# Neighbourhood attention in pairs of heads: two heads' scores on two row tiles, values stationary in two column tiles, probabilities normalised before they are turned

## The chip, the core and the metric

The program runs on one core of a Trainium2 chip. The metric is the device time of one launch in microseconds. Shares, waits and rows come from one profiled execution of the kernel before.

## What is computed

A trunk of four layers over 256 tokens of width 1024, all in float32: state-space mixer, short convolution, neighbourhood attention, state-space mixer, each followed by a squared-ReLU MLP of width 4096 and each sub-layer by a layer norm. The change lies in the attention of the third layer. There the tokens form a grid of 4 rows by 64 columns, there are 16 heads of 64 features, and a query attends to 16 columns of all four rows:

```python
def na_mixer(x, w_qkv, rpb, w_out):
    qkv = (x @ w_qkv).reshape(bsz, rows, GRID_W, 3, NA_HEADS, NA_HEAD_DIM)
    q = qkv[:, :, :, 0] * (NA_HEAD_DIM ** -0.5)
    k = qkv[:, :, :, 1]
    v = qkv[:, :, :, 2]
    ...
    bias = rpb[:, dr_idx[:, None, None, :, None], dc_idx[None, :, :, None, :]]
    bias = jnp.where(in_win[None, None, :, :, None, :], bias.astype(jnp.float32), -jnp.inf)
    def one(t):
        ...
        s = jnp.einsum('rcqhd,rcikhd->hrcqik', qb, kg).astype(jnp.float32) + bias
        p = jax.nn.softmax(s.reshape(shp[:4] + (shp[4] * shp[5],)), axis=-1).reshape(shp)
        o = jnp.einsum('hrcqik,rcikhd->rcqhd', p.astype(vs.dtype), vg)
        return o.reshape(rows * GRID_W, NA_HEADS * NA_HEAD_DIM)
    return lax.map(one, (q, k, v)) @ w_out
```

## The kernel before

Weights stream through in units of 128x2048 numbers. SyncE loads a unit into one of 3 raw buffers, ScalarE copies it to w_high in a rounded float32 form (fp32r), VectorE subtracts to get w_low (the rest), and TensorE multiplies with high and low parts (three matmuls for one product). There are 4 split buffers: the split of unit u waits until unit u-4 has been used, and `result(u)` on ScalarE and VectorE first does the splits up to unit u+3 and then waits for unit u's product. Each engine has its own instruction queue, executed in order and written out by hand; semaphores tie them together.

The attention stage takes the 1024 columns of q, k and v in four blocks of four heads (units q, k, v for each block; v first in block 0), and then four units "no" of the output projection, which accumulate in the four y banks of PSUM. Besides those there are two acc banks, used in turn by the projections of q, k and v, and two inner banks.

For a head, TensorE runs `scores` (q of 128 positions stationary, 64 features contracted, moving 160 keys; twice, for the two halves z of the grid's columns), VectorE adds the bias, takes the maximum and negates it (`biased`, up to L1937), ScalarE writes exp and its sum (`exponents`, L1438) into prob_b (in the tensor xsT, two buffers, a head's number mod 2), TensorE turns the probabilities (`turn_probs`, L1022), ScalarE copies them to SBUF (`keep_probs`, L1449, probT_b in the tensor conv, two buffers), and TensorE mixes the values (`mix_values`, L1033: turned probabilities stationary, 64 features of v moving). ScalarE scales the result by the inverse sum (`scale_out`, L1459) into o_b. After four heads TensorE turns the outputs (`turn_out`, L1047) and ScalarE and VectorE write the high and low part of the operand of the output projection (`out_high` L1468, `out_low` L1950).

TensorE's order for head h is scores(h), dense(h), turn_probs(h-1), mix_values(h-2), and turn_out after heads 7, 11 and 15. dense(h) is a share of the projections: 2, 2, 1, 1 halves of a unit for the heads of a block, for blocks 1 to 3 while heads 0 to 11 run; then half units of "no" 0 and 1 for heads 12 to 15. ScalarE's order is exponents(h), then `keep_qkv` for each unit that dense(h) completed (splits up to u+3, then a copy to ring_a, ring_b or ring_c), from head 14 the split of a further unit, then keep_probs(h-1), scale_out(h-2), out_high. VectorE's is biased(h), the splits, sum_inverse(h-1) (L1942), out_low.

The banks for scores, turned probabilities, mixed values and turned outputs are taken in turn from a ring: inner 0 and 1 and y 0 to 3 up to head 11, inner 0 and 1 and acc 0 and 1 from head 12. Each taking waits until the bank's last content has been read (`take`, called at L551). At head 12 the acc banks are marked as free once qkv_done has reached 12, that is after the copy of the last v. The wait for the probability buffer stands in `exponents`:

```python
                        act.wait_ge(s_max, h + 1)
                        if h >= 2:

                            act.wait_ge(pt_ready, h - 1)
```

## Time and profile before

| | us |
|---|---|
| median of 3 runs | 1497.29 |
| the runs | 1497.29, 1500.34, 1493.65 |
| span of the profiled execution, first to last instruction | 1494.3 |
| TensorE busy in it | 1431.1 (96%) |
| VectorE busy | 999.5 (67%) |
| ScalarE busy | 770.8 (52%) |
| GpSimd busy | 197.1 (13%) |

No other time of the profiled execution is recorded than its span; the runs were timed apart from it.

PE in the profile is TensorE's matmuls, PEld its weight loads, DVE VectorE, ACT ScalarE, POOL GpSimd. Matmuls are pipelined: the duration shown of one reaches past the start of the next, so what a stream costs is read from the distance of its starts. A float32 product is carried out as two instructions each with a weight load, a float32 turning and an fp32r product as one.

### The profile page before, as it was taken

What the parts mean: (1) busy time and instruction counts of PE and PEld (TensorE: products, weight loads), DVE (VectorE), ACT (ScalarE), POOL (GpSimd) and SP (SyncE); (2) the same over time, 40 slices, a digit from 0 to 9 for tenths busy, and PEclk for the clock granted to TensorE, in tenths of its full rate; (3) what the DMA queues carried; (4) which work ended last, traced back from release to release, by engine and by line L of the source; (5) the groups of instructions that cost most, each with busy time, mean ns of one, the idle gap of its engine ahead of it and who ended that gap; (6) DMA issues with size and microseconds to landing.
All of it is one profiled execution on the core that took longest, in us unless ns stands there. A gap on an engine that the chain in (4) does not pass through costs nothing. (4 is left out here: it accounts for less than half of the span.)

```text
span 1494.3 us, 24586 instructions
## 1 busy us (share of the span) xinstructions
PE 1431.1 (96%) x9723; PEld 1325.6 (89%) x9723; DVE 999.5 (67%) x1229; ACT 770.8 (52%) x1105; POOL 197.1 (13%) x245
## 2 busy tenths in 40 slices
PE   7899998999999999999999999999998999999996
PEld 7889997989989989998899889998988999899995
DVE  5899899555487575555744465456789898955554
ACT  4786775344434334444455535443577777454441
POOL 2223222622320000000000000000033121200000
PEclk9999999999999999999999999999999999999998
DMA  8666554666666454556553245645657564555550
GB/s 242 201 197 225 168 172 141 177 191 211 209 199 222 155 192 168 198 176 208 184 166 113 86 141 179 215 170 178 197 170 227 173 191 144 169 179 188 198 197 28
DMA packets 198192, 266.96 MB, mean 179 GB/s; under 512 B 11768, under 2 KB 167824, under 8 KB 198080
## 3 DMA queue, kind: packets, MB, share of 16 engines
q1 hardware_dynamic: 188720, 237.72, 48.0%
q0 software_dynamic: 9200, 27.55, 6.1%
q8 instruction: 78, 1.28, 0.4%
q14 instruction: 34, 0.28, 0.1%
q10 hardware_dynamic: 160, 0.13, 0.0%
HBM read 264.19 MB, written 1.18 MB: 178 GB/s over the span
## 5 line engine op out<-in xcount | busy, mean ns | idle before, releaser
L587 PE MATMUL acc<-xT,w_high 128*128 128x256 f32 x3264 | 599.9, 286 | 3.4 <-DVE w_low L1527 3.4
L1527 DVE TENSOR_TENSOR w_low<-raw,w_high 128x2048 fp32r<-128x2048 f32 (+1 forms) x226 | 512.1, 2275 | 89.4 <-ACT w_high L1119 55.0
L1119 ACT ACTIVATE w_high<-raw 128x2048 fp32r<-128x2048 f32 (+1 forms) x226 | 427.1, 1896 | 208.4 <-DMA raw<-in_ffn_w_in 82.4
L587 PEld LDWEIGHTS acc<-xT,w_high 128*128 128x128 f32 x3264 | 515.7, 193 | 8.7 <-issue 4.9
L587 PE MATMUL acc<-xT,w_low 128*128 128x256 f32 x1632 | 464.0, 284 | 0.0
L739 PE MATMUL y<-w_high,opT 128*128 128x512 f32 x1408 | 398.1, 392 | 1.1 <-ACT w_high L1119 1.0
L587 PEld LDWEIGHTS acc<-xT,w_low 128*128 128x128 f32 x1632 | 315.4, 193 | 0.0
L739 PEld LDWEIGHTS y<-w_high,opT 128*128 128x128 f32 x1408 | 260.0, 189 | 52.4 <-ACT w_high L1119 1.1
L739 PE MATMUL y<-w_low,opT 128*128 128x512 f32 x704 | 223.4, 391 | 0.0
L1546 DVE TENSOR_TENSOR opT<-conv,opT 128x512 fp32r<-128x512 f32 x56 | 39.2, 701 | 264.9 <-issue 238.0
L608 PE MATMUL acc<-w_high,xT 128*128 128x256 f32 (+1 forms) x928 | 177.4, 293 | 9.5 <-DVE xT L1591 9.5
L608 PEld LDWEIGHTS acc<-w_high,xT 128*128 128x128 f32 x928 | 150.4, 199 | 13.0 <-issue 12.7
L739 PEld LDWEIGHTS y<-w_low,opT 128*128 128x128 f32 x704 | 132.6, 188 | 28.4
L608 PE MATMUL acc<-w_low,xT 128*128 128x256 f32 (+1 forms) x464 | 134.2, 289 | 0.0
L430 POOL TENSOR_TENSOR small<-small,minus_half 128x1 f32<-128x1 f32 x16 | 15.9, 993 | 827.0 <-DVE small L1567 827.0
L1162 ACT ACTIVATE conv<-acc 128x512 f32<-128x512 f32 x60 | 35.9, 598 | 147.2 <-PE acc L587 133.0
L1663 DVE SCALAR_TENSOR_TENSOR conv<-conv_pad,ssd_par,conv 128x256 f32<-128x256 f32 x256 | 107.1, 489 | 4.4 <-ACT conv L1193 4.4
L608 PEld LDWEIGHTS acc<-w_low,xT 128*128 128x128 f32 x464 | 92.2, 199 | 0.0
L1149 ACT ACTIVATE xT<-inner 128x512 fp32r<-128x512 f32 x32 | 18.1, 596 | 98.9 <-PE inner L709 98.6
L453 POOL TENSOR_TENSOR ring_a<-ring_b,decay_to_end 128x512 f32<-128x512 f32 x16 | 27.6, 1727 | 161.0 <-ACT ring_b L1249 156.8
L453 POOL TENSOR_TENSOR ring_b<-ring_b,own_token 128x512 f32<-128x512 f32 x16 | 44.3, 2771 | 32.2 <-DVE own_token L1714 32.2
L526 POOL DMA_DIRECT2D E<-in_na_rpb x64 | 34.1, 539 | 95.6 <-ACT conv L1162 94.5
(221 smaller groups left out, 1196.6 us busy)
## 6 DMA issues: line engine op xcount, KB each, us to landing
raw<-in_ffn_w_in SPq DMA_DIRECT2D x128, 512.0 KB, 4.7
raw<-in_ffn_w_out SPq DMA_DIRECT2D x128, 512.0 KB, 4.4
raw<-in_ssd_w_in SPq DMA_DIRECT2D x96, 512.0 KB, 5.3
E<-cumsum_dram POOLq DMA_DIRECT2D x32, 512.0 KB, 6.1
raw<-in_ssd_w_out SPq DMA_DIRECT2D x32, 512.0 KB, 4.4
raw<-in_sc_w_in SPq DMA_DIRECT2D x24, 512.0 KB, 4.8
raw<-in_na_w_qkv SPq DMA_DIRECT2D x24, 512.0 KB, 4.7
raw<-in_sc_w_out SPq DMA_DIRECT2D x8, 512.0 KB, 4.5
```

What stands on the lines that cost most here:

```text
L430: nc.gpsimd.tensor_tensor(small[:, 2 + t:3 + t], small[:, t:t + 1], half_neg[:, 0:1], ALU.pow).then_inc(rstd_done, 1)
L453: return nc.gpsimd.tensor_tensor(spread(dst, shape), spread(tri_b[:, n % 2, :], shape), factors, ALU.mult)
L526: pool.dma_start(dst, src).then_inc(window_landed[h % WINDOW_BUFS], 16)
L587: mm = nc.tensor.matmul(bank[:, c * SEQ:(c + 1) * SEQ][:, span], w[:, col:col + P], xT[:, k, low, span], start=(k == 0 and part == 0), sto ...
L608: mm = nc.tensor.matmul(bank[:, t * width:(t + 1) * width], xT[:, k, low, t * P:(t + 1) * P], w[:, k * width:(k + 1) * width], start=(k == ...
L739: mm = nc.tensor.matmul(Y[t][c][:, :], opT[:, o % ACTS, low, k, t * P:(t + 1) * P], w[:, k * D + c * 512:k * D + (c + 1) * 512], start=(fi ...
L1119: nc.scalar.activation(w_high[:, u % SPLIT, c0:k * c], raw[:, u % RAW, c0:k * c], ACT.Copy).then_inc(w_high_done, 1)
L1149: nc.scalar.activation(xT[:, 4 * half:4 * half + 4, 0, t * P:(t + 1) * P], bank[:, :].rearrange("p (k c) -> p k c", k=4), ACT.Copy).then_i ...
L1162: nc.scalar.activation(conv[:, o % 2, :, :], views(bank[:, :]), ACT.Relu).then_inc(relu_done, 1)
L1527: V.tensor_tensor(w_low[:, u % SPLIT, c0:k * c], raw[:, u % RAW, c0:k * c], f(w_high[:, u % SPLIT, c0:k * c]), ALU.subtract).then_inc(w_lo ...
L1546: V.tensor_tensor(low, src, high, ALU.subtract).then_inc(op_low, 1)
L1663: ins = V.scalar_tensor_tensor(out=y, in0=pad[:, c % 2, i, q:q + SEQ], scalar=tap(j, q, ct), in1=y, op0=ALU.mult, op1=ALU.add)
```

## The change

Heads go in pairs p = 0 to 7. `scores(p)` takes two banks and issues for each z head 2p (rows 0 to 63 of the array) and head 2p+1 (rows 64 to 127). `mix_values(p)` now holds v (64 columns) stationary and moves 256 positions of the turned probabilities, head 2p into output partitions 0 to 63 and head 2p+1 into 64 to 127 of one bank. `turn_out`, `scale_out` and o_b go. The inverse sum is multiplied into the probabilities on VectorE before they are turned (`normalised`), and turn_probs waits for that instead of for the exponents. `out_high` and `out_low` run once for a pair on half an operand. dense(p) has 4, 2, 4, 2, 4, 2 half units and then twice the two halves of "no" 0 and 1. The order of the three queues is written anew by pairs; `exponents` and `biased` keep their waits except that `biased` no longer waits for o_done.

```diff
--- before.py
+++ after.py
@@ -120,16 +120,17 @@
     return units, subs
+PAIRS = NAH // 2
 def attention_order():
     halves = [(what, b, part) for b in range(1, 4) for what in QKV_ORDER[1] for part in range(2)]
-    share = (2, 2, 1, 1) * 3
...
+    plan = [[halves.pop(0) for _ in range(n)] for n in (4, 2) * 3]
+    return plan + [[("no", b, part) for part in range(2)] for b in range(2)]
+ATT_DENSE = attention_order()
 def silu_count(kind, m):
@@ -274,7 +275,8 @@
         qkv_done = sem("qkv_done")
         s_ready, s_biased, s_max, p_done = sem("s_ready"), sem("s_biased"), sem("s_max"), sem("p_done")
-        pt_ready, pt_done, o_ready, o_done = sem("pt_ready"), sem("pt_done"), sem("o_ready"), sem("o_done")
+        pt_ready, pt_done, o_ready = sem("pt_ready"), sem("pt_done"), sem("o_ready")
+        o_half_high, o_half_low = sem("o_half_high"), sem("o_half_low")
         bias_done, prob_zeroed, p_scale = sem("bias_done"), sem("prob_zeroed"), sem("p_scale")
         act_step, dve_step, pool_step = sem("act_step"), sem("dve_step"), sem("pool_step")
...
@@ -1003,54 +1004,48 @@
                     late_ring = [("i", 0), ("i", 1), ("a", 0), ("a", 1)]
                     pe.wait_ge(y_free, 2 * s)
-                    def scores(h):
-                        blk, hh = h // BLOCK_HEADS, h % BLOCK_HEADS
+                    def scores(p):
+                        blk, c = p // 2, (p % 2) * SEQ
                         pe.wait_ge(qkv_done, 3 * blk + (2 if blk else 3))
-                        bank = inner_bank(("s", h), (s_biased, h + 1), ring)
-                        rows, c = slice(64 * (hh % 2), 64 * (hh % 2) + 64), (hh // 2) * SEQ
-                        k = tri_b[rows, blk % 3, c:c + SEQ].rearrange("p (r c) -> p r c", c=GRID_W)
+                        banks = [inner_bank(("s", h), (s_biased, h + 1), ring) for h in (2 * p, 2 * p + 1)]
                         for z in range(2):
-                            mm = nc.tensor.matmul(bank[:, z * KEYS:(z + 1) * KEYS], tri_a[rows, blk % 3, c + z * P:c + (z + 1) * P],
...
+                            for i in range(2):
+                                rows = slice(NAD * i, NAD * (i + 1))
+                                k = tri_b[rows, blk % 3, c:c + SEQ].rearrange("p (r c) -> p r c", c=GRID_W)
+                                mm = nc.tensor.matmul(banks[i][:, z * KEYS:(z + 1) * KEYS], tri_a[rows, blk % 3, c + z * P:c + (z + 1) * P],
+                                                      k[:, :, col0[z]:col0[z] + KCOLS], start=True, stop=True)
+                                if z:
+                                    mm.then_inc(s_ready, 1)
+                    def turn_probs(p):
+                        for h in (2 * p, 2 * p + 1):
+                            pe.wait_ge(p_scale, h + 1)
+                            bank = inner_bank(("pt", h), (pt_done, h + 1), ring)
+                            for t in range(NT):
+                                for z in range(2):
+                                    mm = nc.tensor.transpose(bank[:, t * SEQ + z * P:t * SEQ + (z + 1) * P],
+                                                             prob_b[h % 2][:, z * SEQ + t * P:z * SEQ + (t + 1) * P], ident[:, :])
+                            mm.then_inc(pt_ready, 1)
+                    def mix_values(p):
+                        blk, c = p // 2, p % 2
+                        o = n["op"] + blk
+                        pe.wait_ge(qkv_done, 3 * blk + 3)
+                        pe.wait_ge(pt_done, 2 * p + 2)
+                        bank = inner_bank(("o", p), (op_low, o + 1) if c else (o_half_low, blk + 1), ring)
                         for t in range(NT):
-                            for z in range(2):
...
+                            for i in range(2):
+                                v0 = t * COLS + (2 * c + i) * NAD
+                                mm = nc.tensor.matmul(bank[NAD * i:NAD * (i + 1), 0:SEQ], tri_c[:, blk % 3, v0:v0 + NAD],
+                                                      probT_b[i][:, t * SEQ:(t + 1) * SEQ], start=(t == 0), stop=(t == NT - 1))
                         mm.then_inc(o_ready, 1)
...
-                    def dense(h):
-
-                        for what, blk, part in ATT_DENSE[h]:
+                    def dense(plan):
+                        for what, blk, part in plan:
                             if what == "no":
                                 out_half(s, names[(what, blk)], part, blk == 0)
                             else:
@@ -1059,35 +1054,40 @@
                     banks = {}
                     for what in "qk":
                         project(names[(what, 0)], range(NT))
-                    for h in range(NAH):
-                        if h == 12:
+                    for p in range(PAIRS - 1):
+                        if p == 6:
                             ring = late_ring
                             for b in range(2):
                                 freed[("a", b)] = (qkv_done, 12)
-                        scores(h)
...
+                        scores(p)
+                        dense(ATT_DENSE[p])
+                        if p >= 1:
+                            turn_probs(p - 1)
+                        if p >= 2:
+                            mix_values(p - 2)
+                    scores(PAIRS - 1)
+                    dense(ATT_DENSE[PAIRS - 1][:1])
+                    turn_probs(PAIRS - 2)
+                    mix_values(PAIRS - 3)
+                    dense(ATT_DENSE[PAIRS - 1][1:])
+                    turn_probs(PAIRS - 1)
+                    mix_values(PAIRS - 2)
                     out_half(s, names[("no", 2)], 0, False)
-                    turn_out(3)
+                    mix_values(PAIRS - 1)
                     out_half(s, names[("no", 2)], 1, False)
                     tail(s, [names[("no", 3)]])
-                if kind in ("ffn", "conv"):
+                if kind != "ssd":
                     n["op"] += FFN // COLS if kind == "ffn" else 4
-        def reversed_tokens(bank):
+        def in_token_order(bank):
             ap = bank[:, :]
-            return bass.AP(ap.tensor, ap.offset + SEQ - 1, [list(ap.ap[0]), [SEQ, 2], [-1, SEQ]])
+            return bass.AP(ap.tensor, ap.offset + SEQ - 1, [list(ap.ap[0]), [-QCOLS, ROWS], [-P, 2], [-1, QCOLS]])
+        def by_grid(operand):
+            return operand.rearrange("p (r z c) -> p r z c", r=ROWS, z=2)
         def tap(j, q, ct):
@@ -1413,7 +1413,7 @@
                         bank = result(names[(what, b)])
                         if b == 3:
-                            act.wait_ge(o_ready, BLOCK_HEADS)
+                            act.wait_ge(o_ready, 2)
                         dst = {"q": tri_a, "k": tri_b, "v": tri_c}[what][:, b % 3, :]
                         if what == "q":
                             for c in range(2):
@@ -1441,52 +1441,40 @@
                                                        accum_out=att[:, h % 4, 4 + z:5 + z])
                         ins.then_inc(p_done, 1)
-                    def keep_probs(h):
...
-                    base = n["turned"]
+                    def keep_probs(p):
+                        for h in (2 * p, 2 * p + 1):
+                            act.wait_ge(pt_ready, h + 1)
+                            if p:
+                                act.wait_ge(o_ready, p)
+                            nc.scalar.activation(probT_b[h % 2], inner_of[("pt", h)][:, :], ACT.Copy).then_inc(pt_done, 1)
+                    def out_high(p):
+                        c = p % 2
+                        act.wait_ge(o_ready, p + 1)
+                        nc.scalar.activation(by_grid(operand(n["op"])[:, c, :]), in_token_order(inner_of[("o", p)]),
+                                             ACT.Copy).then_inc(op_high if c else o_half_high, 1)
+                        n["op"] += c
                     for what in QKV_ORDER[0]:
                         keep_qkv(what, 0)
-                    for h in range(NAH):
-                        exponents(h)
-                        for what, b, part in ATT_DENSE[h]:
+                    for p in range(PAIRS):
+                        for h in (2 * p, 2 * p + 1):
+                            exponents(h)
+                        for what, b, part in ATT_DENSE[p]:
                             if part and what != "no":
                                 keep_qkv(what, b)
-                        if h >= 14:
...
+                        if p >= 6:
+                            split_to(names[("no", 3)] + p - 6)
+                        if p >= 1:
+                            keep_probs(p - 1)
+                        if p >= 2:
+                            out_high(p - 2)
+                    keep_probs(PAIRS - 1)
+                    out_high(PAIRS - 2)
+                    out_high(PAIRS - 1)
             split_to(len(units) - 1)
@@ -1927,43 +1915,46 @@
                         if h >= 2:
                             dve.wait_ge(p_done, h - 1)
-                        if h >= 4:
-
-                            dve.wait_ge(o_done, h - 3)
                         V.scalar_tensor_tensor(out=sc, in0=inner_of[("s", h)][:, 0:2 * KEYS], scalar=float(NAD) ** -0.5,
                                                in1=bias_all[:, h, :], op0=ALU.mult, op1=ALU.add).then_inc(s_biased, 1)
                         dve.wait_ge(s_biased, h + 1)
                         chain(V.tensor_reduce(st[:, 0:2], views(sc), AX.X, ALU.max))
                         V.tensor_scalar(st[:, 2:4], st[:, 0:2], -1.0, None, ALU.mult).then_inc(s_max, 1)
-                    def sum_inverse(h):
+                    def normalised(h):
                         st = att[:, h % 4, :]
                         dve.wait_ge(p_done, h + 1)
-                        V.reciprocal(st[:, 6:8], st[:, 4:6]).then_inc(p_scale, 1)
-
...
+                        chain(V.reciprocal(st[:, 6:8], st[:, 4:6]))
+                        shape = [[SEQ + col0[1] - col0[0], 2], [GRID_W, ROWS], [1, KCOLS]]
+                        probs = spread(prob_b[h % 2][:, col0[0]:col0[0] + 1], shape)
+                        V.tensor_tensor(probs, probs, spread(st[:, 6:7], [[1, 2], [0, ROWS], [0, KCOLS]]), ALU.mult).then_inc(p_scale, 1)
+                    def out_low(p):
+                        c, o = p % 2, n["op"]
+                        dve.wait_ge(*((op_high, o + 1) if c else (o_half_high, p // 2 + 1)))
                         low, high = operand(o)
-                        V.tensor_tensor(low, reversed_tokens(inner_of[("op", o)]), high, ALU.subtract).then_inc(op_low, 1)
+                        V.tensor_tensor(by_grid(low[:, c, :]), in_token_order(inner_of[("o", p)]), by_grid(high[:, c, :]),
+                                        ALU.subtract).then_inc(op_low if c else o_half_low, 1)
+                        n["op"] += c
                     for what in QKV_ORDER[0]:
                         split_to(names[(what, 0)] + 3)
-                    for h in range(NAH):
-                        biased(h)
-                        for what, b, part in ATT_DENSE[h]:
+                    for p in range(PAIRS):
+                        for h in (2 * p, 2 * p + 1):
+                            biased(h)
+                        for what, b, part in ATT_DENSE[p]:
                             if part and what != "no":
                                 split_to(names[(what, b)] + 3)
-                        if h >= 14:
...
+                        if p >= 6:
+                            split_to(names[("no", 3)] + p - 6)
+                        for h in (2 * p, 2 * p + 1):
+                            normalised(h)
+                        if p >= 2:
+                            out_low(p - 2)
+                    out_low(PAIRS - 2)
+                    out_low(PAIRS - 1)
             for t in range(NT):
                 norm(len(subs) - 1, t)
```

## Rows read from the trace of the kernel before

**Rows 1.** The page: busy time and share of TensorE's matmuls.

```profile
PE 1431.1 (96%) x9723; PEld 1325.6 (89%) x9723; DVE 999.5 (67%) x1229; ACT 770.8 (52%) x1105; POOL 197.1 (13%) x245
```

**Rows 2.** Busy us by engine over the stage, instructions, granted clock, DMA share, GB/s.

```profile
746.70:855.70 109.00, 107.61 (x776) 99.35 (x777) 47.98 (x81) 59.85 (x141) 0.00 (x0) 0.98 0.38 126
```

**Rows 3.** Timeline of TensorE, a head's step: start, length, line, output and inputs, count.

```profile
803.63 0.28 PE L587 MATMUL acc<-xT,w_high 128*128 128x256 f32 x1
803.75 0.28 PE L587 MATMUL acc<-xT,w_low 128*128 128x256 f32 x1
803.87 0.60 PE L1022 MATMUL inner<-ident,xsT 128*128 128x128 f32 x4
804.30 1.00 PE L1033 MATMUL inner<-ring_c,conv 128*128 128x64 f32 x8
805.24 0.81 PE L1013 MATMUL y<-ring_b,ring_a 64*128 64x160 f32 x4
```

**Rows 4.** Timeline of TensorE, turned outputs, scores, a half unit of output projection.

```profile
796.74 0.61 PE L1047 MATMUL y<-ident,gate 128*128 128x128 f32 x4
...
823.26 0.61 PE L1047 MATMUL y<-ident,square 128*128 128x128 f32 x4
823.80 0.81 PE L1013 MATMUL inner<-ring_b,ring_a 64*128 64x160 f32 x4
824.54 0.73 PE L739 MATMUL y<-w_high,opT 128*128 128x512 f32 x2
...
827.39 0.60 PE L1022 MATMUL inner<-ident,xsT 128*128 128x128 f32 x4
```

**Rows 5.** The scores' line: length in ns of one (least, median, most).

```profile
L1013 PE MATMUL y<-ring_b,ring_a x32: 296/296/400, 753.5 to 818.8; 64*128 64x160 f32 x32
```

**Rows 6.** Timeline of TensorE in the last layer: float32 products of 256 moving columns.

```profile
1262.17 1.03 PE L884 MATMUL inner<-ring_a,E 128*128 128x256 f32 x4
1263.04 1.89 PE L897 MATMUL inner<-ring_b,E 128*128 128x64 f32 x16
```

**Rows 7.** Timeline of ScalarE over a head's exponents, a split, copies.

```profile
800.78 0.43 ACT L1438 ACTIVATE xsT<-tanh,softmax_stats 128x160 f32<-128x160 f32 x1 [2.33 <-DVE softmax_stats L1937]
...
801.62 1.90 ACT L1119 ACTIVATE w_high<-raw 128x2048 fp32r<-128x2048 f32 x1
804.07 0.66 ACT L1423 ACTIVATE ring_a<-acc 128x256 f32<-128x256 f32 x2 [0.55 <-PE acc L587]
804.61 0.60 ACT L1449 ACTIVATE conv<-inner 128x512 f32<-128x512 f32 x1
```

**Rows 8.** Timeline of VectorE over a split, an inverse and a head's bias and maximum.

```profile
803.60 2.29 DVE L1527 TENSOR_TENSOR w_low<-raw,w_high 128x2048 fp32r<-128x2048 f32 x1 [2.86 <-ACT w_high L1119]
805.81 0.15 DVE L1942 RECIPROCAL softmax_stats<-softmax_stats 128x2 f32<-128x2 f32 x1
806.08 0.49 DVE L1933 SCALAR_TENSOR_TENSOR tanh<-y,E 128x320 f32<-128x320 f32 x1
...
807.13 0.17 DVE L1937 TENSOR_SCALAR softmax_stats<-softmax_stats 128x2 f32<-128x2 f32 x1
```

**Rows 9.** Timeline of TensorE at the stage's end; in brackets idle time and its releaser.

```profile
845.51 1.08 PE L1033 MATMUL acc<-ring_c,conv 128*128 128x64 f32 x8 [0.90 <-ACT conv L1449]
846.85 1.08 PE L1033 MATMUL acc<-ring_c,conv 128*128 128x64 f32 x8 [0.26 <-issue]
848.08 0.81 PE L739 MATMUL y<-w_high,opT 128*128 128x512 f32 x2
...
852.50 0.60 PE L1047 MATMUL inner<-ident,square 128*128 128x128 f32 x4
852.85 0.71 PE L739 MATMUL y<-w_high,opT 128*128 128x512 f32 x2
```

**Rows 10.** Timeline of TensorE in the last layer, behind its longest idle stretch.

```profile
1151.43 0.41 PE L897 MATMUL inner<-ring_b,E 128*128 128x64 f32 x2 [3.04 <-DVE E L1708]
```

**Rows 11.** By stretch as in rows 2: the clock behind those two idle stretches.

```profile
849.00:852.00 3.00, 3.00 (x8) 2.31 (x8) 0.00 (x0) 0.00 (x0) 0.00 (x0) 0.51 0.91 316
1152.00:1159.00 7.00, 7.00 (x36) 7.00 (x36) 6.97 (x9) 2.17 (x2) 3.75 (x3) 0.52 0.82 295
```

More of the change, by code:

```diff
@@ L120, in plan_units @@
     return units, subs
+PAIRS = NAH // 2
 def attention_order():
     halves = [(what, b, part) for b in range(1, 4) for what in QKV_ORDER[1] for part in range(2)]
-    share = (2, 2, 1, 1) * 3
-    plan = [[halves.pop(0) for _ in range(n)] for n in share]
-    plan += [[("no", b, part)] for b in range(2) for part in range(2)] + [[]]
-    return plan, {7: 0, 11: 1, 15: 2}
-ATT_DENSE, ATT_TURN = attention_order()
+    plan = [[halves.pop(0) for _ in range(n)] for n in (4, 2) * 3]
+    return plan + [[("no", b, part) for part in range(2)] for b in range(2)]
+ATT_DENSE = attention_order()
 def silu_count(kind, m):
@@ L1965, in _ @@
-                    sum_inverse(NAH - 1)
-                    out_low()
+                        if p >= 6:
[6 more added lines that the diff above has]
+                    out_low(PAIRS - 1)
             for t in range(NT):
```

84 lines of the change are left out of this document (removed).

## The prediction, with its working

> **What bounds the kernel now.** I read first the page's busy shares: TensorE is busy 96% of the span [rows 1]. Then the table by stretch over the attention stage, from the first scores (746.78) to the last unit of the output projection (855.7): TensorE is busy 107.6 of 109.0 us at 0.98 of its clock, ScalarE 59.9, VectorE 48.0 [rows 2]. So the stage costs what TensorE has to issue, and the other two have slack in sum. The question is whether they have it at the right moment. Then TensorE's timeline. The step of one head, between two half projections, is: turn the probabilities (803.87), mix the values (804.30), scores (805.24) [rows 3], and 0.74 later the next projection (823.80 to 824.54 [rows 4]): 0.43 + 0.94 + 0.74 = 2.11 us. The block of four heads, from one turning of the outputs to the next, takes 823.26 - 796.74 = 26.52 us, the turning itself 0.54 [rows 4]. Three units of projection at 48 matmuls x 0.12 = 5.76 us (starts 0.12 apart at 803.63 and 803.75 [rows 3]) are 17.3 and four head steps 8.4; the 0.3 left I put down to a slow start of the projection behind each of the four scores, 0.08 each. At the end of the stage there is idle time and a clock drop (below).
>
> **TensorE's work, before and after.** Times of an instruction are distances between starts.
> Scores: the four of a head last 0.81 together and one lasts 0.30, so the last is issued 0.51 after the first; the first lasts 0.40 and holds 0.1 more than the others [rows 4, 5], so the steady distance is (0.51 - 0.1)/3 = 0.137. The projection follows 0.23 after the last, 0.09 more than steady. I book 0.1 + 0.09 + 0.08 = 0.27 for going to the 64-row form and back, and 4 x 0.137 = 0.55 of streaming: 0.82 a head, 1.64 a pair. After: one change of form for 8 instructions. In a row 8 x 0.137 + 0.27 = 1.37. If the two row tiles run side by side, order a,a,b,b,a,a,b,b, they stream in 5 slots (0.68), but 8 loads of 128 weight columns remain, and the mix, with 64 moving columns only, shows that those are taken every 0.94/8, some 0.11 without the change of form at its end. So S = 0.88 + 0.27 = 1.15 as the value taken, 0.95 to 1.37 the bounds.
> Mix: 8 a head in 0.94, 1.88 a pair [rows 3]. After: 8 a pair with 256 moving columns; the nearest row is the 256-column float32 product of the other stage, 0.87 for 4 = 0.217 each [rows 6]. In a row 1.73 + 0.09 for the new change of form = 1.82; side by side 5 x 0.217 + 0.09 = 1.17. No row shows two tiles at once. I take M = 1.17, since the two halves share neither array columns nor output partitions, and keep 1.82 as the bound.
> Turning the probabilities stays (0.87 a pair). Turning the outputs goes: 4 x 0.53 = 2.1.
> If nothing waited, eight pairs would fall from 0.87 + 1.88 + 1.64 = 4.39 to 0.87 + 1.17 + 1.15 = 3.19 (9.6 us), 2.1 more go, and with the idle time and the clock drop at the end (1.2 and 1.6, below) it is 14 us, about 1%.
> The Trainium skill ("TensorE: Matmul & The Clock Gate", Part 3) has two such tiles start 4 ns apart, in agreement with the value taken; were the weight loads side by side as well, S would be 0.95 and the sum below 1.0 us less. "TensorEngine Tiling (Array Packing)" (Key Properties) says that a change of tiling mode drains the engine, which speaks against the change; the 0.27 is what the trace makes of it.
>
> **The queue that decides.** exponents(h) at L1430 waits for s_max and for head h-2's probabilities to be turned (two buffers). Before, turn_probs(h-2) stands ahead of scores(h), so this wait is never late. After, turn_probs(p-1) stands behind dense(p), so ScalarE, in order, stands from its arrival at exponents(2p) until dense(p) has ended. Behind it are queued the copies of dense(p)'s q, k and v out of the accumulators, the weight splits L1119, the probability copies and out_high. VectorE waits for those splits (w_low L1527), and behind them stand its new normalised() and out_low.
> ScalarE's durations [rows 7]: exponents of a head 0.84 to the next instruction, w_high 1.90, q copy 0.66, probability copy 0.60. VectorE's [rows 8]: w_low 2.29, starting 0.08 after w_high's end (801.62 + 1.90); bias, maximum and negation 1.22; reciprocal 0.15, started 0.08 before the end of w_low, and I let the next instruction start that much early everywhere. The new multiplication is 128x320 like L1933: 0.49 (between 0.2 and 0.7, I take the same size); with the reciprocal and two hand-overs 0.68 a head. out_low on half a tile is about 0.37, and out_high 0.38 (estimates: ring_a's two copies of 128x256 take 0.66 [rows 7]). ScalarE loses 32 scalings of 0.3 and VectorE gains 16 x 0.53: in sum nothing on the path.
>
> **Even pairs 2 and 4** (two units, then one). T is the end of dense(p). The first head is turned at T+0.60, exponents run 0.63 to 2.31, w_high to 4.2, q's copy to 4.8. dense(p+1) takes the accumulator of q (two banks), so it starts at T+4.9, where TensorE has work only to 0.87 + 1.17 + 1.15 = 3.2. VectorE: w_low 4.3 to 6.6, and 6.7 to 9.0, then both normalisations to 10.2, ahead of dense(p+1)'s end at T+10.66. No second wait. So pair p to p+1 costs 10.66 whatever M and S are; p+1 to p+2 costs 3.19 + 11.52 = 14.7.
> **Pair 5 to 6.** The late ring has four banks. Before, 35 banks had been taken ahead of scores(12), which got inner0 (823.80 [rows 4], and acc0, acc1 come two on); now it is 26, nine fewer, so scores(6) gets acc1 and inner0. acc1 waits for the copy of v3 (qkv_done 12), inner0 for the copy of head 8's probabilities. T = end of dense(5): VectorE's s_max of heads 10 and 11 at 0.95 and 2.1, exponents to 2.9, w_high to 4.8, v3 5.35, head 8 at 5.83. Scores at 5.9 instead of 2.04. Then dense(6) starts the y banks and y00 holds the output of pair 3 until out_low(3), which stands behind w_low (4.9 to 7.2) and two normalisations (8.4): 8.8. Scores end at 7.0.
> **Pair 6 to 7.** T = end of dense(6). exponents to 2.3, w_high 4.2, copy of head 10 at 4.7: scores(7) takes that bank, so 4.8 instead of 2.04. Then half projection (2.85), turn, mix, half projection: 13.7. turn_probs(7) needs normalised(14): exponents(15) end 11.35, w_high 13.25, w_low 15.6, normalised 16.2. Start 16.3, second head 16.9 to 17.4. Mix 18.5, half 21.4, mix 22.5, half 25.4.
> **Sum.** scores(0) at 746.78; dense(0) ends 746.78 + 1.05 + 11.52 = 759.35; dense(1) + 1.15 + 5.76 = 766.3; dense(2) + 0.87 + 1.15 + 11.52 = 779.8; dense(3) + 10.66 = 790.5; dense(4) + 14.7 = 805.2; dense(5) + 10.66 = 815.8; dense(6) + 8.8 + 5.7 = 830.3; the last unit starts + 25.4 = 855.7. Before it starts at 852.85 + 2.85 = 855.7 [rows 9]. The 14 us are gone: 0.0. What follows is alike (out_high(7), out_low(7) are done 2 us ahead).
>
> **The clock.** Before, idle time of 0.90 and 0.26 at the end of TensorE's is followed by 849 to 852 at 0.51, that is 1.2 GHz [rows 9, 11]; twelve matmuls took 848.08 to 852.50 = 4.4 where 2.85 is usual (824.54 to 827.39 [rows 4]): 1.6 us. Elsewhere an idle stretch of 3.04 us is followed by 7 us at 0.52 [rows 10, 11]. The new ones by my schedule: 3.9 and then 1.8 (pair 6), 2.8 (pair 7), 2.6 (turn 7), and 1.7 twice (pairs 3 and 5). I count three drops of the short kind for the long ones and one for the two of 1.7, of which the rows read say nothing: 4 x 1.6 - 1.6 that goes = +4.7 (bounds: 0 and 15, below).
> Forecast: span 1494.3 + 4.7 = 1499.0; the median of the runs lies 3.0 above this execution's span, so 1497.3 + 4.7 = 1502.
>
> **Rivals.**
> 1. The gain arrives: ScalarE isn't late, because the exponents find a free buffer sooner than I read. For: the sums of [rows 2]. Against: the wait at L1430 is in the code and unchanged. 1497.3 - 14, less some waits: 1486. Chance 0.12.
> 2. The tiles don't overlap (the change doesn't do what it says). With S = 1.37 and M = 1.82, five scores outside the waits cost +0.22 each, three mixes +0.65: +3.1, at the same clock: 1505. For: every row of the trace has these instructions in a row. Chance 0.23.
> 3. The clock as the bound, and slower: the 7 us at 0.52 [rows 11] lose 3.3 us. If each of five new stretches costs that, 5 x 3.3 - 1.6 = +15: 1512. It decides once the low clock holds over 15 us more in the stage. Chance 0.13.
> The forecast itself, 0.0 with a few drops: 0.50. The rest, 0.02, is spread.
>
> **How the numbers follow.** 0.5% is 7.5 us, about what a measurement of this kernel can tell from no change. Range 1494.5 to 1509: from the forecast without any new drop (1495.7) and a little less, over rival 2 with a spare drop or two, to part of rival 3; it leaves out rival 1 and most of 3. Faster than 1489.8: 0.11. Slower than 1504.8: 0.13 from rival 3, 0.14 from rival 2 (half of it and more lies above), 0.06 from the upper part of the forecast: 0.33. Within: 0.56.
>
> **What would show it.** On ScalarE's timeline the first exponents of a pair (xsT, L1438's successor) start right behind the first turning, with an idle stretch before them released by TensorE. TensorE's waits list the copies of ring_a and ring_b or ring_c, and conv (probabilities) before scores, and VectorE's opT before dense(6). dense(3) and dense(5) start about 4.9 after the unit before. The eight mix instructions of a pair take near 1.1 us side by side, 1.7 in a row. VectorE's multiplication is near 0.49. The clock by stretch has dips after pairs 5, 6 and 7. The forecast is wrong if dense(p+1) doesn't wait, if dense(6) starts under 5 us after dense(5), or if the clock stays at 2.4 GHz throughout.

## The result, and the profile after

| kernel | median, us | runs | smallest and largest |
|---|---|---|---|
| before | 1497.05 | 10 | 1492.82, 1500.34 |
| after | 1503.81 | 10 | 1498.77, 1507.79 |

The ratio is 1.005, with a 95% interval of 1.0036 to 1.0064: the change makes the kernel slower by half a per cent, 6.8 us. The forecast was 1502.0. Two single executions ran far slower than the others of the same kernel (one of the four with four buffers, 1564.67 us, and one of the kernel before, 2824.81); no median or ratio here rests on them.

The page of the changed kernel answers to [rows 1]: span, then busy us and share of each engine.

```profile
span 1502.5 us, 24380 instructions
PE 1427.9 (95%) x9643; PEld 1317.1 (88%) x9643; DVE 1007.3 (67%) x1249; ACT 762.1 (51%) x1077; POOL 196.2 (13%) x245
```

TensorE has less to do (1431.1 before) and the span is 8.2 longer. The table by stretch says where. The first line runs from the first scores to the start of the last unit of the output projection; before, that took 855.7 - 746.78 = 108.9. The columns are the stretch, its length, busy time of PE, PEld, DVE, ACT and POOL with instructions, then the granted clock, the DMA share and GB/s.

```profile
748.70:864.00 115.30, 100.57 (x696) 87.83 (x697) 55.39 (x101) 50.62 (x112) 0.00 (x0) 0.91 0.35 117
786.10:789.60 3.50, 3.50 (x18) 3.50 (x19) 3.45 (x2) 3.29 (x5) 0.00 (x0) 0.52 0.19 40
813.40:816.90 3.50, 3.50 (x20) 3.50 (x19) 3.42 (x4) 2.50 (x5) 0.00 (x0) 0.52 0.39 114
827.00:834.00 7.00, 5.81 (x14) 4.60 (x15) 3.05 (x10) 0.00 (x0) 0.00 (x0) 0.51 0.48 150
840.70:847.70 7.00, 6.46 (x20) 5.01 (x21) 5.90 (x12) 1.14 (x3) 0.00 (x0) 0.52 0.45 149
```

The stage is 6.4 us longer, and in it TensorE stands idle for 14.7 us, where it was busy 107.6 of 109.0 [rows 2]. Its clock is at 0.91 over the stage, because of four stretches at about 0.52, that is 1.2 GHz; before, there was one of 3.4 us [rows 11]. (Of the rest of the 8.2, 1.9 us lie ahead of the stage, in layers whose code is the same.)

TensorE's timeline at the places where it waits. The columns are start, duration, line, output and inputs, tile and shape, count, and in brackets the idle time before and what ended it.

```profile
781.08 1.04 PE L1028 MATMUL y<-ident,xsT 128*128 128x128 f32 x8
782.04 1.08 PE L1042 MATMUL y<-conv,ring_c 128*64 128x256 f32 x8
783.06 0.81 PE L1016 MATMUL inner<-ring_b,ring_a 64*128 64x160 f32 x8
785.91 0.70 PE L609 MATMUL acc<-w_high,xT 128*128 128x256 f32 x2 [2.04 <-ACT ring_a L1423]
...
819.77 1.04 PE L1028 MATMUL inner<-ident,xsT 128*128 128x128 f32 x8
820.74 1.08 PE L1042 MATMUL y<-conv,ring_c 128*64 128x256 f32 x8
825.13 0.37 PE L1016 MATMUL acc<-ring_b,ring_a 64*128 64x160 f32 x1 [3.31 <-ACT conv L1451]
828.19 0.77 PE L740 MATMUL y<-w_high,opT 128*128 128x512 f32 x1 [2.25 <-DVE opT L1938]
...
841.24 1.44 PE L1016 MATMUL inner<-ring_b,ring_a 64*128 64x160 f32 x8 [2.83 <-ACT conv L1451]
855.00 0.66 PE L1028 MATMUL inner<-ident,xsT 128*128 128x128 f32 x4 [2.26 <-DVE xsT L1931]
```

First comes the end of dense(2): pair 1 is turned (781.08), pair 0 mixed (782.04), pair 3 scored (783.06), and then there is 2.04 us of nothing, until ScalarE has copied q out of the accumulator that dense(3) takes; dense(5) has the same 2.04. scores(6) waits 3.31 for a copy of the probabilities and dense(6) 2.25 for out_low, scores(7) waits 2.83, and the last turning 2.26 for the new multiplication. ScalarE's timeline shows why it is late with q:

```profile
781.77 0.43 ACT L1438 ACTIVATE xsT<-tanh,softmax_stats 128x160 f32<-128x160 f32 x1 [8.33 <-PE y L1028]
783.43 1.89 ACT L1119 ACTIVATE w_high<-raw 128x2048 fp32r<-128x2048 f32 x1
785.23 0.63 ACT L1423 ACTIVATE ring_a<-acc 128x256 f32<-128x256 f32 x2
...
788.04 1.07 ACT L1451 ACTIVATE conv<-y 128x512 f32<-128x512 f32 x2
```

It stood 8.33 us at the exponents of pair 2, held by the turning of pair 1 (L1028), which TensorE issues behind dense(2). Only then come the exponents, a split and the copy of q, one behind the other.

### The profile page after: what moved, and what is told of

Same layout as the page of the kernel before. It is cut to its first block and busy times, and to the rows that moved or that the text cites. A ratio compares the mean times of both kernels' runs of the same rounds, so it can differ in the third digit from the quotient of the medians.

```text
span 1502.5 us, 24380 instructions
## 1 busy us (share of the span) xinstructions
PE 1427.9 (95%) x9643; PEld 1317.1 (88%) x9643; DVE 1007.3 (67%) x1249; ACT 762.1 (51%) x1077; POOL 196.2 (13%) x245
## 5 line engine op out<-in xcount | busy, mean ns | idle before, releaser
L609 PE MATMUL acc<-w_high,xT 128*128 128x256 f32 (+1 forms) x928 | 182.5, 298 | 13.9 <-DVE xT L1579 9.3
L609 PEld LDWEIGHTS acc<-w_high,xT 128*128 128x128 f32 x928 | 155.3, 205 | 17.1 <-issue 12.0
```

The source lines that it names most:

```text
L609: mm = nc.tensor.matmul(bank[:, t * width:(t + 1) * width], xT[:, k, low, t * P:(t + 1) * P], w[:, k * width:(k + 1) * width], start=(k == ...
```

## The experiments

The kernel before, run again beside each group of them, had medians of 1496.0 to 1496.4. The stage in the table is from the first scores to the start of the last half unit ahead of the last unit, with TensorE's idle time in it and the stretches of its profile at the low clock.

| kernel | median, us (runs) | ratio to before (95%) | stage, us | idle, us | low clock, us |
|---|---|---|---|---|---|
| before | 1497.05 (10) | | 106.07 | 1.2 | 3.4 |
| after | 1503.81 (10) | 1.0050 (1.0036 to 1.0064) | 112.48 | 14.7 | 3.4, 3.4, 6.8, 6.8 |
| four buffers | 1484.35 (3) | 0.9919 (0.9899 to 0.9939) | 92.25 | 3.1 | none |
| turned first | 1485.44 (4) | 0.9924 (0.9908 to 0.9940) | 93.13 | 3.7 | none |
| no product | 1500.21 (10) | 1.0019 (1.0005 to 1.0032) | 106.92 | 12.5 | 3.4, 3.4, 6.8 |
| filled | 1495.51 (10) | 0.9996 (0.9981 to 1.0010) | 105.19 | 4.2 | none |
| not in turn | 1488.15 (4) | 0.9936 (0.9917 to 0.9954) | 93.22 | 3.7 | none |
| four turned | 1483.93 (4) | 0.9917 (0.9899 to 0.9935) | 92.0 | 2.4 | none |
| single heads, late wait | 1502.6 (4) | 1.0041 (1.0025 to 1.0057) | 110.94 | 4.8 | 6.8 |
| copies first | 1488.91 (4) | 0.9946 (0.9930 to 0.9962) | 98.88 | 6.7 | 3.4, 3.4 |

The theory is the prediction's: the pair's gain on TensorE is there, and it is lost because the turning of pair p-1 stands behind dense(p) and holds ScalarE at the exponents. The rivals are VectorE's multiplication as the new bound, the clock, and tiles that don't stream side by side.

### Four probability buffers

The changed kernel with two more buffers for the probabilities before they are turned, so that the exponents of pair p need pair p-2 turned, not p-1.

```diff
-prob_b = [xsT[:, n, ...] for n in range(2)]
+prob_b = [xsT[:, n, ...] for n in range(2)] + [gate[:, :], sq[:, :]]
...
-    if h >= 2:
-        act.wait_ge(pt_ready, h - 1)
+    if h >= 4:
+        act.wait_ge(pt_ready, h - 3)
     else:
-        act.wait_ge(prob_zeroed, 1)
+        act.wait_ge(prob_zeroed, 1 + h // 2)
```

(prob_b is indexed by h % 4 throughout; GpSimd zeroes the two new ones ahead of the stage.)

> The changed kernel with four probability buffers instead of two (the two tiles that held the outputs before), so that the exponents of pair p wait for pair p-2 to be turned, not for pair p-1. Theory A (ScalarE held at the exponents until dense(p) has ended): dense(3) and dense(5) start about 2.8 us after the unit before instead of 4.8, scores(6) 2 to 3 us after dense(5) instead of 5.4, dense(6) within 3 us instead of 8.4, no or one clock drop in the stage; the stage loses about 22 us against the changed kernel (3.6 twice at pairs 3 and 5, 8.1 at pair 6, 7.2 behind it), so about 1482, under the kernel before by 15. Theory B (VectorE's new multiplication is what comes late): the waits stay, under 3 us of change, about 1502. Theory C (banks of the ring are what comes late): gain only at pairs 3 and 5, 7 us, about 1497.

1484.35 us, 19.5 under the changed kernel where about 22 was expected. The stretch of the stage, one of the waits that TensorE has left in it (us in total, times, longest; none is longer) and the place of the 2.04:

```profile
750.30:845.40 95.10, 91.94 (x696) 80.85 (x697) 56.92 (x101) 52.36 (x112) 0.00 (x0) 1.00 0.43 145
PE y L744 <- DVE opT L1942: 0.9, 1, 0.9
...
784.69 0.81 PE L1020 MATMUL inner<-ring_b,ring_a 64*128 64x160 f32 x8
785.43 0.50 PE L613 MATMUL acc<-w_high,xT 128*128 128x256 f32 x2
```

The stage falls from 115.30 to 95.10, the clock is full throughout, dense(3) follows its scores in 0.74. All that the buffers change is when ScalarE may begin; so what it waited for carried the whole loss, the idle time and the clock with it. It doesn't say yet whether buffers are needed.

### The turning ahead of the projection

```diff
 scores(p)
-dense(ATT_DENSE[p])
 if p >= 1:
     turn_probs(p - 1)
+dense(ATT_DENSE[p])
```

(For the last pair likewise: turn_probs(PAIRS - 2) ahead of the half unit.)

> The changed kernel, two buffers, but TensorE turns the probabilities of pair p-1 right behind scores(p), ahead of dense(p), instead of behind it. Theory A: the exponents are free early again although no buffer is added; two new short waits (turning needs the products of a pair whose split is late: about 1 us at single units, 2 us at the last pair), in sum 15 to 20 us less than the changed kernel, 1484 to 1489. Theory B (the multiplication or VectorE's backlog): turning waits earlier and longer, so slower than the changed kernel, over 1504. Theory C (banks): as now within 3 us.

```profile
746.50:842.50 96.00, 92.32 (x696) 80.59 (x697) 56.31 (x101) 52.92 (x112) 0.00 (x0) 1.00 0.43 143
PE inner L1028 <- DVE xsT L1931: 1.3, 2, 0.7
PE acc L1016 <- ACT conv L1451: 0.8, 1, 0.8
...
781.67 0.81 PE L1016 MATMUL inner<-ring_b,ring_a 64*128 64x160 f32 x8
782.42 1.09 PE L1028 MATMUL y<-ident,xsT 128*128 128x128 f32 x8
783.26 0.48 PE L609 MATMUL acc<-w_high,xT 128*128 128x256 f32 x2
```

With two buffers as in the changed kernel, 1485.44 us, alike with four buffers (their intervals in the table overlap). The turning of pair p-1 is now ahead of dense(p), ScalarE is released a whole projection earlier, and TensorE waits 0.7 at most for the multiplication, since between the scores of a pair and its turning there is still the projection of its own step. The two stages differ by 112.48 - 93.13 = 19.4 us: 11.0 are TensorE's waits (14.7 less 3.7), and the 8.5 that the low clock costs (worked out below) are the rest. Taken a second time, with more rounds:

> The kernel e2_turn_first once more, beside the next one on the same chip. By its trace TensorE's waits in the stage for banks and turned probabilities come to 3.7 us: 1485.5.

1485.19 us (6 runs), ratio 0.9931 (0.9916 to 0.9946). The line moved (and its like for the last pair) is worth 18.4 us against the changed kernel, and the pairs are then 11 us faster than the kernel before.

### Without the multiplication

The changed kernel without VectorE's product of probabilities and inverse sums; the reciprocal alone releases the turning. The normalisation is left out of what it computes.

```diff
-chain(V.reciprocal(st[:, 6:8], st[:, 4:6]))
+V.reciprocal(st[:, 6:8], st[:, 4:6]).then_inc(p_scale, 1)
...
-V.tensor_tensor(probs, probs, spread(...), ALU.mult).then_inc(p_scale, 1)
```

> The changed kernel without the multiplication of the probabilities by the inverse sum on VectorE (the inverse is still taken; the result is therefore not normalised: this part of the computation is left out). VectorE has 16 x 0.49 = 7.8 us less. Theory A: only what stands behind the products gains, dense(6) by about 1 us and the last turning by 1 us; 0 to 3 us in all, 1501 to 1504. Theory B: most of the stalls go, 10 us or more, under 1494.

1500.21 us. TensorE's waits in the stage:

```profile
PE acc L609 <- ACT ring_a L1423: 4.1, 2, 2.0
PE acc L1016 <- ACT conv L1451: 3.3, 1, 3.3
PE inner L1016 <- ACT conv L1451: 2.8, 1, 2.8
PE inner L1028 <- DVE softmax_stats L1928: 1.8, 1, 1.8
PE y L740 <- DVE opT L1937: 0.5, 1, 0.5
```

The waits on ScalarE stand unchanged at 4.1, 3.3 and 2.8; only VectorE's two go down, 2.25 to 0.5 and 2.3 to 1.8. The low stretch behind scores(7) is gone as well, though the wait of 2.83 before it stands. The multiplication costs 3.6 us by the medians and 112.48 - 106.92 = 5.6 in the stage of the two traces: 2.2 of waits, the rest nearly all the clock (dense(6) takes 7.26 for 8.17, scores(7) and the half unit behind them 3.60 for 6.47). Most of the 14.7 us of waits stay without it, so it isn't the cause. The time is 0.8 us below the range that I had expected.

### The idle time filled

The changed kernel with the same scores and mixes issued again where it stands idle, ahead of their signals: scores of pairs 3, 5 and 6 four times, mixes of pairs 3 and 4 four times and of pair 5 three times.

```diff
-for z in range(2):
+for again in range({3: 3, 5: 3, 6: 3}.get(p, 0), -1, -1):
+  for z in range(2):
...
-            if z:
+            if z and not again:
...
-for t in range(NT):
+for again in range({3: 3, 4: 3, 5: 2}.get(p, 0) + 1):
+  for t in range(NT):
```

> The changed kernel with TensorE's idle stretches filled by repeating work that changes nothing: scores of pairs 3, 5 and 6 issued three more times, mixes of pairs 3 and 4 three more times, of pair 5 twice more, before they are signalled. All waits stay. It measures the clock alone. If the low clock follows TensorE's idle time and costs what the trace of the changed kernel suggests (dense(3) and dense(5) 1.6 us too long each, dense(6) 2.4, the half unit behind scores(7) 2.2), the stage is 6 to 8 us shorter than in the changed kernel, 1496 to 1498. If the clock falls for another reason or its loss lies beside waits, no change: 1503, or more where the filling delays work.

1495.51 us. The stretch of the stage, and the filled place of pair 3:

```profile
747.20:855.30 108.10, 103.89 (x833) 90.34 (x833) 56.14 (x101) 51.01 (x112) 0.00 (x0) 1.00 0.38 127
...
781.57 2.44 PE L1017 MATMUL inner<-ring_b,ring_a 64*128 64x160 f32 x32
784.42 0.50 PE L609 MATMUL acc<-w_high,xT 128*128 128x256 f32 x2 [0.41 <-ACT ring_a L1425]
...
790.27 1.04 PE L1029 MATMUL y<-ident,xsT 128*128 128x128 f32 x8
```

More work (833 matmuls for 696), and 1503.81 - 1495.51 = 8.3 us less time. The waits are those of the changed kernel: dense(3) still starts 4.83 after the end of dense(2), when ring_a is copied. What differs is the clock, 1.00 for 0.91: dense(3) takes 790.27 - 784.42 = 5.85, where it took 7.35. That prices the clock by itself at 8.3 us by the medians. In the stage of the two traces it is 112.48 - 105.19 = 7.3, and there the filling isn't free: the repeated mixes outlast the wait, and scores(6) and scores(7) start 0.6 us later each (5.98 for 5.36 and 5.49 for 4.88 after the projection ahead of them). Without these 1.2 us the clock's price is 8.5. The whole stage at full clock, 108.10 with those 1.2 us in it, stands beside 108.9 of before, which has a drop of its own in it.

### The two tiles not in turn

The kernel with the turning first, its matmuls a,a,a,a,b,b,b,b instead of a,a,b,b,a,a,b,b.

```diff
-for z in range(2):
-    for i in range(2):
+for i in range(2):
+    for z in range(2):
...
-for t in range(NT):
-    for i in range(2):
+for i in range(2):
+    for t in range(NT):
```

> The kernel e2_turn_first (no long waits, so that TensorE's work shows in the time) with the two heads of a pair issued one after the other instead of in turn: all scores of one head, then of the other, and the same for the mixed values. If it is the turns that let the two tiles stream side by side (four slots of 0.137 and four of 0.217 instead of eight), matmuls start in order and the other head can begin only beside the last one of the first: 7 slots instead of 4, 0.41 a pair for the scores and 0.65 for the mix, 8.5 us over e2_turn_first: 1494. If TensorE doesn't need the turns, or if waits bound it, no change: 1485.

```profile
748.78 0.40 PE L1016 MATMUL inner<-ring_b,ring_a 64*128 64x160 f32 x1 [0.69 <-ACT ring_b L1427]
748.80 0.40 PE L1016 MATMUL y<-ring_b,ring_a 64*128 64x160 f32 x1
749.02 0.30 PE L1016 MATMUL inner<-ring_b,ring_a 64*128 64x160 f32 x1
749.04 0.30 PE L1016 MATMUL y<-ring_b,ring_a 64*128 64x160 f32 x1
749.16 0.30 PE L1016 MATMUL inner<-ring_b,ring_a 64*128 64x160 f32 x1
749.17 0.30 PE L1016 MATMUL y<-ring_b,ring_a 64*128 64x160 f32 x1
749.30 0.30 PE L1016 MATMUL inner<-ring_b,ring_a 64*128 64x160 f32 x1
749.31 0.30 PE L1016 MATMUL y<-ring_b,ring_a 64*128 64x160 f32 x1
```

I had expected it to lose the overlap, and it missed: in the records the two heads (banks inner and y) still start in pairs, 10 to 20 ns apart, and the stage takes 93.22 beside 93.13. The median, 1488.15, is 2.7 above the other's, and their intervals overlap; as the stages are alike I don't put this down to the order. So this kernel is no control without overlap, and none of the runs is one. What shows overlap is the rate: eight instructions of scores are issued in four steps, 0.76 us to the projection behind them for 0.74 to 0.75 in turn, and the eight of a mix take 1.02 for 1.01.

### More buffers behind the turning too

```diff
-probT_b = [conv[:, n, ...] for n in range(2)]
+probT_b = [conv[:, n, ...] for n in range(2)] + [gate[:, :], sq[:, :]]
...
-    if p:
-        act.wait_ge(o_ready, p)
-    nc.scalar.activation(probT_b[h % 2], ...)
+    if p >= 2:
+        act.wait_ge(o_ready, p - 1)
+    nc.scalar.activation(probT_b[h % 4], ...)
```

> The kernel e2_turn_first with four buffers for the turned probabilities (the two tiles free since the outputs are no longer turned), so that the copy of pair p needn't wait for the mix of pair p-1. Theory: the 0.85 us waits of scores(6) and scores(7) for a bank, behind that copy, and part of the 0.55 us one at the end go: 1 to 2 us less than e2_turn_first, 1483.5 to 1484.5. If the banks are held by something else: 1485.5.

1483.93 us, 1.5 under the turning first alone, with the stage at 92.0 for 93.13. Repeated:

> The kernel e6_four_turned once more. If its shorter waits (1.7 us in sum by its trace instead of 3.7) are what made it 1.5 us faster than e2_turn_first, the difference stays at 1.5 to 2: 1483.7. If that was scatter between runs, both come out alike.

1485.25 us (6 runs), ratio 0.9927 (0.9913 to 0.9941), beside 0.9931 for the other, run at the same time. (The waits of the four turned buffers come to 2.4 us, as in the table, not to 1.7.) In time the two are alike; the buffers bring nothing that can be told, and the version with one line moved is the one to keep.

### Single heads with the late wait

The kernel before, its exponents waiting for the head ahead instead of the one before that: the changed kernel's late wait without its pairs.

```diff
-if h >= 2:
-    act.wait_ge(pt_ready, h - 1)
+if h >= 1:
+    act.wait_ge(pt_ready, h)
+    act.wait_ge(prob_zeroed, 1)
```

> The kernel before with one wait added: the exponents of head h wait until head h-1 is turned, which on TensorE stands behind dense(h), the place that the wait has in the changed kernel. If the late wait costs by itself, in any form of the stage: 5 us or more over the kernel before, over 1501. If it costs only together with what pairs put behind it (two heads' exponents, two units' splits and copies in a row, while the next projection waits for the first copy), a head's exponents (0.84 us) and one split and copy (2.5) fit into the 5 us of a step, and the time is that of the kernel before within 2 us: 1496 to 1499.

```profile
800.88 0.60 PE L1047 MATMUL y<-ident,gate 128*128 128x128 f32 x4
827.41 0.61 PE L1047 MATMUL y<-ident,square 128*128 128x128 f32 x4
830.66 0.47 PE L739 MATMUL y<-w_high,opT 128*128 128x512 f32 x1 [1.91 <-ACT conv L1450]
...
852.00:862.00 10.00, 8.29 (x34) 7.30 (x34) 3.02 (x4) 4.07 (x10) 0.00 (x0) 0.66 0.50 168
```

1502.6 us, more than the 1496 to 1499 I had expected. The block of four heads takes 827.41 - 800.88 = 26.53, as in [rows 4] to a hundredth: while q, k and v are projected, the late wait alone costs nothing. At the end of the stage it does: waits of 1.9, 1.7 and 1.2 come in and 6.8 us of low clock behind them, and the stage takes 110.94 for 106.07, 4.9 more. (The medians differ by 6.6; the trace has the rest outside the stage, 4.2 more ahead of it and 2.2 less behind it, in code that is the same.) So the pairs' stall in the middle needs both, the late wait and the pairs. That it is twice the work of exponents and projection behind the wait that makes it is an argument; no run takes one of the two away from single heads or pairs by itself.

### ScalarE's copies first

The changed kernel with ScalarE's copies of q, k and v ahead of the pair's exponents.

```diff
 for p in range(PAIRS):
-    for h in (2 * p, 2 * p + 1):
-        exponents(h)
     for what, b, part in ATT_DENSE[p]:
         if part and what != "no":
             keep_qkv(what, b)
+    for h in (2 * p, 2 * p + 1):
+        exponents(h)
```

> The changed kernel with one swap in ScalarE's order: the splits and copies of dense(p)'s units ahead of the exponents of pair p, not behind them. Buffers, banks, TensorE's and VectorE's order stay. Theory A: dense(3) and dense(5) no longer wait (3.6 us each with the clock), scores(6) about 3 us after dense(5) instead of 5.4 and dense(6) 4.3 instead of 8.4; the waits of scores(7) and of the last turning stay. 11 to 13 us under the changed kernel, about 1491. If the exponents' place isn't the cause, or if now the normalised probabilities are late: 1500 or more.

```profile
782.75 0.81 PE L1016 MATMUL inner<-ring_b,ring_a 64*128 64x160 f32 x8
783.49 0.39 PE L609 MATMUL acc<-w_high,xT 128*128 128x256 f32 x1
815.32 0.37 PE L1016 MATMUL acc<-ring_b,ring_a 64*128 64x160 f32 x1 [1.03 <-ACT conv L1451]
816.63 0.70 PE L740 MATMUL y<-w_high,opT 128*128 128x512 f32 x2 [0.50 <-DVE opT L1938]
```

1488.91 us, 14.9 under the changed kernel, for the 11 to 13 expected. dense(3) follows its scores in 0.74, scores(6) waits 1.03 instead of 3.31 and dense(6) 0.50 instead of 2.25. The waits of pair 7 (2.8) and of the last turning (2.3) stay, because no copies of q, k and v stand there, with a low stretch of 3.4 us behind each. The same cause is taken away at a third place, and only where this edit reaches it.

## Why the prediction held, step by step

**The queue** held. The places of the stall and its sizes come out as worked. Each is counted from the end of the projection: of dense(2) and dense(4) for the first row, of dense(5) (819.77) for scores(6) and dense(6), of dense(6) (836.36) for the rest:

| step | predicted | measured |
|---|---|---|
| dense(3), dense(5) start | +4.9 | +4.83, +4.84 |
| scores(6) | +5.9 | +5.36 |
| dense(6) | +8.8 | +8.42 |
| scores(7) | +4.8 | +4.88 |
| last turning | +16.3 | +18.6, of it 2.9 low clock |
| last unit | +25.4 | +27.7, of it 2.9 low clock |
| stage without low clock, against 108.9 | 0.0 | 115.3 - 8.5 - 108.9 = -2.1 |

Scores(6) come earlier than worked because ScalarE's exponents end 2.36 after dense(5) (822.13 on its timeline) and not 2.9: VectorE's maxima of heads 10 and 11, taken at 0.95 and 2.1, are both done by 0.61.

VectorE's multiplication, for which no row stood, was taken at 0.49 and is that, beside a split of 2.29 and out_low, whose estimate was 0.37:

```profile
824.11 2.29 DVE L1515 TENSOR_TENSOR w_low<-raw,w_high 128x2048 fp32r<-128x2048 f32 x1 [3.74 <-ACT w_high L1119]
826.51 0.49 DVE L1931 TENSOR_TENSOR xsT<-xsT,softmax_stats 128x320 f32<-128x320 f32 x1
827.52 0.42 DVE L1938 TENSOR_TENSOR opT<-y,opT 128x256 fp32r<-128x256 f32 x1
```

**TensorE's work** was taken too dear. Scores of a pair take 0.74 to the projection behind them (783.49 - 782.75 in the kernel with the copies first), and the projection still takes 5.85 where 48 x 0.12 is 5.76; in the prediction's booking, which counts that 0.09 with the scores, they take 0.83, where 1.15 was taken and 0.95 was the lower bound. The step at fault is that eight weight loads remain in a row at 0.11 each: the loads of the two tiles go side by side as well (in the records of the loads the pairs start at 748.70 and 748.71, 748.81 and 748.82), and eight instructions take four slots of 0.137, not the five behind the 0.95. The change of form is 0.83 - 4 x 0.137 = 0.28, as booked (0.27). The Trainium skill ("TensorE: Matmul & The Clock Gate", Part 3) has each array tile with its own weights; the trace agrees. The mix takes 783.06 - 782.04 = 1.02 for 1.17, the turning 0.96 for 0.87. Where the projection behind the scores starts when q's copy is done, none of it moves the time; elsewhere it does, by about 1 us in all: dense(2) ends 781.08 - 748.70 = 32.4 after the first scores, worked 33.0, and the step from pair 4 to 5 is 807.59 - 793.26 = 14.3, worked 14.7. It is half of the 2.1 us by which the stage's schedule is shorter than worked. Where little waits it counts fully: the turning first gains 12.9 us in the stage with 3.7 of idle time left, near the 14 that the prediction had for an unstalled schedule.

**The clock** is the term of the sum that was mis-sized, twice over. Predicted: 4 drops of 1.6 (1.57 unrounded) less the one of before = 4.7. The subtraction is wrong. The 0.0 was got by comparing with 855.7, and the drop of before lies inside that time (4.42 for 2.85 [rows 9]); a schedule that ends at the same point at full clock has already used up what that drop gives back. The four drops had to be added whole, 6.3, and the forecast was then 1503.6. The second fault is the size. Against the same pieces in the filled kernel, dense(3) and dense(5) took 7.35 and 7.34 for 5.85 and 5.84, 1.5 more each; dense(6) 8.17 for 5.53, 2.6; scores(7) and the half unit behind them 6.47 for 3.60, 2.9. That is 8.5 for the 6.3. The idle stretches of 2.04 after pairs 3 and 5, one drop for the two of which the sum counted, were both followed by one. And where two idle stretches stand near each other (3.31 and 2.25) the low clock lasted 6.8 us, as after the 3.04 of [rows 10, 11], not 3.4; the same length came behind the 2.83 of pair 7, while the last wait of 2.26 had none behind it. A wait's length alone doesn't settle it: the same 2.83 was followed by 3.4 us in the kernel with the copies first and by none in the one without the product.

**What made the sum come near.** In the stage the forecast has 0.0 + 4.7 and the traces -2.1 + 8.5 = 6.4. The clock's term was 3.8 too small, and the schedule 2.1 too long, which hid over half of it: that 1502.0 is within 2 us of 1503.81 is in part luck. That the gain is lost, where and by what, is not.

**The rivals.** The gain that arrives (1486) did not, but it is what the pairs give once the turning is moved: 1485.4. The tiles without overlap (1505) come near the measured time for a wrong reason: two heads' mixes in 1.02 leave no room for a row of eight at 0.217. The clock as the bound (1512; 1513.8 without the subtraction that is wrong there too) met its point, with 20.4 us at the low clock for 3.4, 17 more; its price was too high, since two of the stretches are short and part of the long ones is spent waiting, so that 20.4 us cost 8.5 and not half of five times seven. Of slower by over 0.5% and within 0.5%, the result stands on the edge: +0.50% by the ratio, and 1503.81 is below the 1504.8 of the text.

Not settled: before and after differ by 1.9 us ahead of the stage, in the same code; and behind the stage the kernel with the turning first takes 2.3 us more than before and that with four buffers 1.8 less. Single profiles don't tell whether that is more than scatter.

## What to carry to other kernels

Saving an engine's work gains nothing when the work regrouped around it holds another engine's queue: ask for each in-order queue what its first waiting instruction needs, and what stands behind it. When steps are merged into larger ones with the same two buffers, a release that stood a small step ahead comes to stand a large one behind; move the release forward, as here by one line for 18 us, ahead of buying buffers. And when a schedule puts idle time on TensorE, add the clock to its price: here the low clock cost 8.3 us, more than the whole difference between the two kernels. When a schedule is compared with a measured time, see first which losses that time already holds, or one of them is taken off twice.

## What was new of the hardware

- Float32 products in two row tiles or two column tiles streamed side by side, weight loads with them: four slots of 0.137 us for eight instructions of 160 columns, and 1.02 us for eight of 256 columns, the change of form with them. In the records the second tile's starts up to 20 ns behind the first.
- Eight instructions issued tile by tile took the time of eight issued in turn, 0.76 us beside 0.75, and are shown starting in pairs (748.78 and 748.80, 749.02 and 749.04). "TensorE: Matmul & The Clock Gate" (Part 3) of the Trainium skill lets matmuls start in the program's order; these records don't agree with it. Nor does the time: by that order there would be seven slots, 7 x 0.137 = 0.96 us ahead of any change of form. What no run here shows is whether the instructions reached the engine in the order in which the kernel writes them.
- An idle stretch of 2.04 us was followed by 3.4 us at 1.2 GHz at all four places where it occurred (two in the changed kernel, two in the one without the product), and the projection behind it lost 1.5 us each time. Filling the idle time with repeated products kept the clock at 2.4 GHz and returned 8.3 us, 0.55% of the kernel.
